# In odd attention heads the values product by three passes of rounded parts, and the next head's keys ahead of the third scores

## What is computed

```python
kv = (key_ckv @ p["w_ukv"]).reshape(B, M, N_HEADS, QK_NOPE + V_DIM)
k_nope, v = kv[..., :QK_NOPE], kv[..., QK_NOPE:]
...
s = jnp.einsum("bqhd,bkhd->bhqk", qi, k).astype(jnp.float32) * scale
p = jax.nn.softmax(s, axis=-1).astype(v.dtype)
return jnp.einsum("bhqk,bkhd->bqhd", p, v)
```

## Time and profile before

| | |
|---|---|
| median of 3 runs | 2737.5 us (2736.6 to 2740.0) |
| the profiled execution | 2737.6 us, its span 2735.8 us |
| one head in steady order | 17.9 us |
| the eight heads of layer 1, from the first Exp to the end of head 7 | 135.7 us |
| mean granted TensorE clock | 0.993 of full speed |

### The profile page before, as it was taken

The page is one execution under the profiler, slowest core; times in us unless marked ns, Lnnn a source line. Parts: engine busy times, 40 slices in busy tenths (PEclk is TensorE's granted clock), DMA queues, the critical chain, the costliest instruction groups (busy, mean ns, idle before and its releaser), DMA issues. The chain is left out here.

```text
span 2735.8 us, 44480 instructions
## 1 busy us (share of the span) xinstructions
PE 2664.7 (97%) x17686; PEld 2524.1 (92%) x17686; DVE 2092.7 (76%) x2832; ACT 1213.6 (44%) x2002; POOL 626.7 (23%) x327
## 2 busy tenths in 40 slices
PE   5999999999999999999999999999999999999997
PEld 3999999977899999999989999999779999999997
DVE  6978879776567788887888879888665668786876
ACT  5533425556432543343564435355663245343433
POOL 1322412023000124232322413310220003232230
PEclk9999999999999999999999999999999999999999
DMA  6434232211233253423324243322113322222312
GB/s 233 158 119 135 85 124 73 70 44 32 74 128 102 95 170 113 132 99 104 101 99 154 93 133 106 110 62 70 30 37 115 126 83 78 93 80 68 109 47 77
DMA packets 87693, 270.90 MB, mean 99 GB/s; under 512 B 8704, under 2 KB 12544, under 8 KB 87360
## 3 DMA queue, kind: packets, MB, share of 16 engines
q1 hardware_dynamic: 86048, 263.51, 29.3%
q10 hardware_dynamic: 1440, 4.56, 0.5%
HBM read 265.12 MB, written 2.92 MB: 98 GB/s over the span
## 5 line engine op out<-in xcount | busy, mean ns | idle before, releaser
L690 POOL TENSOR_TENSOR sums_raw<-raw_pairs 128x1024 f32<-128x1024 f32 x88 | 238.3, 2708 | 1618.6 <-DVE weights_lo L1822 1032.9
L725 PE MATMUL ps<-h_hi,weights_hi 128*128 128x322 f32 (+1 forms) x1408 | 440.3, 313 | 8.9 <-DVE t_lo L1822 3.1
L729 PE MATMUL ps<-h_hi,weights_lo 128*128 128x322 f32 (+1 forms) x1408 | 437.1, 310 | 0.0
L727 PE MATMUL ps<-h_lo,weights_hi 128*128 128x322 f32 (+1 forms) x1408 | 436.6, 310 | 0.0
L1822 DVE TENSOR_TENSOR weights_lo<-sums_raw,weights_hi 128x1024 fp32r<-128x1024 f32 (+2 forms) x296 | 329.8, 1115 | 57.1 <-ACT weights_hi L1344 27.1
L725 PE MATMUL ps<-t_hi,weights_hi 128*128 128x322 f32 (+1 forms) x1056 | 330.4, 313 | 5.3 <-DVE h_lo L1822 5.3
L725 PE MATMUL ps<-a_hi,weights_hi 128*128 128x320 f32 x1408 | 325.1, 312 | 5.3 <-DVE tmp L2024 3.6
L729 PE MATMUL ps<-t_hi,weights_lo 128*128 128x322 f32 (+1 forms) x1056 | 327.4, 310 | 0.0
L727 PE MATMUL ps<-t_lo,weights_hi 128*128 128x322 f32 (+1 forms) x1056 | 326.3, 309 | 0.0
L727 PE MATMUL ps<-a_lo,weights_hi 128*128 128x320 f32 x1408 | 321.4, 309 | 0.0
L729 PE MATMUL ps<-a_hi,weights_lo 128*128 128x320 f32 x1408 | 321.2, 309 | 0.0
(11 more groups left out here) (288 smaller groups left out, 5750.9 us busy)
## 6 DMA issues: line engine op xcount, KB each, us to landing
raw_pairs<-in_w_up SPq DMA_DIRECT2D x87, 1024.0 KB, 5.0
wm<-in_w_mod SPq DMA_DIRECT2D x72, 512.0 KB, 4.0
raw<-in_w_merge SPq DMA_DIRECT2D x32, 704.0 KB, 4.1
sums_raw<-in_w_down SPq DMA_DIRECT2D x56, 384.0 KB, 3.2
sums_raw<-in_w_down SPq DMA_DIRECT2D x64, 320.0 KB, 3.0
wm<-in_w_mod SPq DMA_DIRECT2D x48, 256.0 KB, 3.0
raw<-in_w_in SPq DMA_DIRECT2D x16, 512.0 KB, 3.5
late_wm<-in_w_mod SPq DMA_DIRECT2D x16, 512.0 KB, 3.5
```

The lines of the kernel that those rows point to most:

```text
L690: nc.gpsimd.tensor_tensor(sums_raw[:, UNIT:3 * UNIT].rearrange("p (s c) -> p s c", s=2), w.rearrange("p (s c) -> p s c", s=2)[:, :, 0:UNIT ...
L725: nc.tensor.matmul(out, whi, v, start=first, stop=False)
L727: nc.tensor.matmul(out, whi, v, start=False, stop=False)
L729: mm = nc.tensor.matmul(out, wlo, v, start=False, stop=last)
```

## The change

Head by head it does the following.

- In odd heads `values(j)` becomes three passes: v1 (values rounded, and ones) x the rounded exponentials, the values' lo part (64 result rows) x the rounded exponentials, and v1 x the exponentials' lo part. It waits for VectorE's subtraction (`s_vxlo`) in place of the Exp.
- In odd heads `exponent(j)` issues two Exps, one to the rounded buffer `ex_parts(h, j)[0]`, one to the float32 buffer `ex[j % 2]`. For j of 2 and more it also waits for `exponent_lo(j - 2)`. `exponent_lo(hd, j)` on VectorE subtracts the rounded from the float32 exponentials. The parts lie in columns of the weight slots that a head's chunk leaves free; for head 7 in q0 and a view over `tmp`.
- `values_lo` on VectorE makes the lo part of an odd head's values from PSUM, before the last maximum of the even head.
- v1 is rounded and has the values first, the ones last, written by ScalarE once a layer; GpSimd's memset of v1 goes. `o_copy` takes its rows accordingly.
- The order of odd heads changes on TensorE (keys and values of the next head ahead of `scores(2)`; `values(j)` after `scores(j + 2)`), on ScalarE (`keys` ahead of the third Exp, `values_copy` ahead of the fourth, `split_queries` after the fourth) and on VectorE (subtractions between the maxima). Even heads keep theirs but for `values_lo`.

```diff
+        with ExitStack() as of_last:
+            last_parts = sb("last_parts", [P, 6 * T + 4], F32R, of_last)
...
-                    v1 = sb("v1", [P, KEYS // P, P], F32, head)
+                    v1 = sb("v1", [P, KEYS // P, P], F32R, head)
...
+        def ex_parts(h, j):
+
+            n = SAMPLE if j < 6 else P
+            if h == HEADS - 1 and j % 2:
+                return q0_hi[:, 0:n], q0_lo[:, 0:n]
+            if h == HEADS - 1:
+                return last_parts[:, 2 * SAMPLE:2 * SAMPLE + n], last_parts[:, 2 * SAMPLE + 2 * T:2 * SAMPLE + 2 * T + n]
+            at = 3 * UNIT * (j % 2) + SLOT - SAMPLE
+            return mix_w_hi[:, at:at + n], mix_w_lo[:, at:at + n]
+
+        def value_lo_parts(h):
+
+            if h == HEADS - 1:
+                return last_parts[:, 2 * SAMPLE + T:2 * SAMPLE + T + 4 * VD],                     last_parts[:, 2 * SAMPLE + T + 4 * VD:2 * SAMPLE + T + 7 * VD]
+            return mix_w_hi[:, HEAD_W:HEAD_W + 4 * VD], mix_w_lo[:, HEAD_W:HEAD_W + 3 * VD]
+
+        def value_lo_done(hd):
+            return hd // 2 * 8 + 1
+
+        def ex_lo_done(hd, j):
+            return hd // 2 * 8 + 2 + j
...
-                for s in range(2):
-                    nc.gpsimd.memset((v0, v1)[s][:, :, (1 - s) * VD:(2 - s) * VD], 1.0).then_inc(s_fill, 1)
-                    pool.wait_ge(s_fill, 7 + 2 * l + s + 1)
+                nc.gpsimd.memset(v0[:, :, VD:2 * VD], 1.0).then_inc(s_fill, 1)
+                pool.wait_ge(s_fill, 7 + l + 1)
...
                 if hd % HEADS and not tail:
                     pe.wait_ge(s_v, hd)
+                    if hd % 2 == 0:
+                        pe.wait_ge(s_vxlo, value_lo_done(hd - 1))
...
-                    pe.wait_ge(s_exp, t0 + j + 1)
-                    out, v_in = (bank(7), ex[j % 2]) if j < 6 else (bank(1 if following else 3, 0, P), ex[j % 2][:, 0:P])
-                    nc.tensor.matmul(out, vals[b][:, j, :], v_in, start=j in (0, 6), stop=j in (5, 6)).then_inc(s_pv, 1)
+                            pe.wait_ge(s_fill, 7 + l + 1)
+                    out = bank(7) if j < 6 else bank(1 if following else 3, 0, P)
+                    if b:
+                        pe.wait_ge(s_vxlo, ex_lo_done(hd, j))
+                        e_hi, e_lo = ex_parts(h, j)
+                        value_lo = value_lo_parts(h)[j // 4][:, j % 4 * VD:(j % 4 + 1) * VD]
+                        nc.tensor.matmul(out, v1[:, j, :], e_hi, start=j in (0, 6), stop=False)
+                        nc.tensor.matmul(out[0:VD], value_lo, e_hi, start=False, stop=False)
+                        nc.tensor.matmul(out, v1[:, j, :], e_lo, start=False, stop=j in (5, 6)).then_inc(s_pv, 1)
+                    else:
+                        pe.wait_ge(s_exp, t0 + j + 1)
+                        v_in = ex[j % 2] if j < 6 else ex[j % 2][:, 0:P]
+                        nc.tensor.matmul(out, v0[:, j, :], v_in, start=j in (0, 6), stop=j in (5, 6)).then_inc(s_pv, 1)
...
+                if b:
+                    if following:
+                        pe.wait_ge(s_rowc, hd + 1)
+                        keys_values(c1 % 2, QT)
+                    scores(2)
+                    values(0)
+                    scores(3)
+                    values(1)
+                    scores(4)
+                    if following:
+                        rough(hd + 1, 0, 2)
+                    values(2)
+                    if following:
+                        rough(hd + 1, 1, 2)
+                        turn_values(hd + 1)
+                        rough(hd + 1, 2, 2)
+                    scores(5)
+                    values(3)
+                    if following:
+                        rough(hd + 1, 3, 2)
+                    scores(6)
+                    values(4)
+                    if following:
+                        rough(hd + 1, 4, 2)
+                    values(5)
+                    values(6)
+                    if following:
+                        maximum_rows(hd + 1)
+                    return
...
+                one_rows = ones[:, 0:VD]
+                nc.scalar.activation(v1[:, :, VD:P], bass.AP(one_rows.tensor, one_rows.offset,
+                                                             [one_rows.ap[0], (0, KEYS // P), (1, VD)]), ACT.Copy)
...
             def o_copy(hd):
                 s = hd % 2
-                o_rows, s_rows = slice(s * VD, (s + 1) * VD), slice((1 - s) * VD, (2 - s) * VD)
+                o_rows = slice(s * VD, (s + 1) * VD)
                 act.wait_ge(s_pv, (hd + 1) * 7)
                 act.wait_ge(s_olo, hd // 2)
-                for dst, rows in ((o32, o_rows), (sums, s_rows)):
+                for dst, rows in ((o32, slice(0, VD)), (sums, slice(VD, P))):
...
+                    if h % 2:
+                        if j >= 2:
+                            act.wait_ge(s_vxlo, ex_lo_done(hd, j - 2))
+                        nc.scalar.activation(ex_parts(h, j)[0], bank(j % 2, 0, n), ACT.Exp)
                     nc.scalar.activation(ex[j % 2][:, 0:n], bank(j % 2, 0, n), ACT.Exp).then_inc(s_exp, 1)
 
                 if following:
                     queries(hd + 1)
                 exponent(0)
                 exponent(1)
+                if h % 2:
+                    weight_hi(2 * mixp + HEADS_C + h + 2)
+                    if following:
+                        keys(hd + 1, mixp, head_chunk(h + 1))
+                    exponent(2)
+                    if following:
+                        values_copy(hd + 1)
+                    exponent(3)
+                    if following:
+                        split_queries(hd + 1)
+                    exponent(4)
+                    if following:
+                        values(hd + 1)
+                    exponent(5)
+                    exponent(6)
+                    if following:
+                        maximum_hi(hd + 1)
+                    o_copy(hd)
+                    if following:
+                        maximum_copy(hd + 1)
+                    return
...
-                for h in range(HEADS):
-                    if h and h % 2 == 0:
+                nc.vector.tensor_copy(k1_lo[NOPE:QK + 2, :], k0_lo[NOPE:QK + 2, :].bitcast(F32)).then_inc(s_krlo, 1)
+                for h in range(0, HEADS, 2):
+                    if h:
                         o_norm(l, h // 2 - 1)
                     weight_lo(c0 + HEADS_C + h + 2)
-                    if h and h % 2 == 0:
+                    if h:
                         o_lo(l, h // 2 - 1)
-                    if h + 1 < HEADS:
-                        split_queries(hd0 + h + 1)
-                        split_keys(hd0 + h + 1)
-                        for u in range(UNITS):
-                            maximum(hd0 + h + 1, u)
-                        maximum_lo(hd0 + h + 1)
+                    split_queries(hd0 + h + 1)
+                    split_keys(hd0 + h + 1)
+                    for u in range(UNITS):
+                        if u == UNITS - 1:
+                            values_lo(hd0 + h + 1)
+                        maximum(hd0 + h + 1, u)
+                    maximum_lo(hd0 + h + 1)
+                    odd, following = hd0 + h + 1, h + 2 < HEADS
+                    exponent_lo(odd, 0)
+                    weight_lo(c0 + HEADS_C + h + 3)
+                    exponent_lo(odd, 1)
+                    exponent_lo(odd, 2)
+                    if following:
+                        split_keys(odd + 1)
+                    exponent_lo(odd, 3)
+                    if following:
+                        maximum(odd + 1, 0)
+                        split_queries(odd + 1)
+                        maximum(odd + 1, 1)
+                    exponent_lo(odd, 4)
+                    if following:
+                        maximum(odd + 1, 2)
+                        maximum(odd + 1, 3)
+                    exponent_lo(odd, 5)
+                    if following:
+                        maximum(odd + 1, 4)
+                    exponent_lo(odd, 6)
+                    if following:
+                        maximum_lo(odd + 1)
...
+            def values_lo(hd):
+                dve.wait_ge(s_v, hd + 1)
+                for to, first, last in zip(value_lo_parts(hd % HEADS), (0, 4), (4, 7)):
+                    ins = lo_of(to.rearrange("p (a n) -> p a n", n=VD),
+                                bank(4, first * VD, last * VD).rearrange("p (a n) -> p a n", n=VD), v1[:, first:last, 0:VD])
+                ins.then_inc(s_vxlo, 1)
+
+            def exponent_lo(hd, j):
+                e_hi, e_lo = ex_parts(hd % HEADS, j)
+                dve.wait_ge(s_exp, hd * 7 + j + 1)
+                lo_of(e_lo, ex[j % 2][:, 0:SAMPLE if j < 6 else P], e_hi).then_inc(s_vxlo, 1)
```

More of the change, by code:

```diff
@@ L368, in build @@
         q_hi, q_lo = [q0_hi, ot_hi[:, OT - 1, :]], [q0_lo, ot_lo[:, OT - 1, :]]
-        k_hi, k_lo, vals = [k0_hi, k1_hi[:]], [k0_lo[:], k1_lo[:]], [v0, v1]
+        k_hi, k_lo = [k0_hi, k1_hi[:]], [k0_lo[:], k1_lo[:]]
```

(36 more changed lines are left out.)

## The result

The changed kernel takes 2761.45 us (median of 5 runs, 2757.24 to 2764.32), the kernel before 2737.5: the ratio is 1.0087, with a 95% interval of 1.0076 to 1.0098. It is slower, as predicted, by 24 us where 28.5 was forecast. The profiled execution took 2759.8 us, its span is 2757.8.

A forecast was written before the change was run, and what follows sets the result against it. TensorE, busy 97% of the span, was taken as the bound. To 2737.6 us came +23.4 (odd heads +15.2, head 7 +6.6, even heads +1.6) and +5.1 for the clock: 2766 us, range 2751 to 2777.

The forecast's parts named there:

- the walk: Step-by-step timing of an odd head across the engines, giving TensorE waits of 1.35, 1.39 and 0.91 us.
- values(5): Third wait of an odd head: VectorE's row of maxima and subtractions ends 16.13, TensorE arrives 15.38; 0.91 us.
- First wait: Odd head, before values(1): second subtraction delayed by GpSimd's rotations at the shared port; 1.35 us.
- Second wait: Odd head, before rough(0): the queries' rounding stands behind the fourth Exp pair, which waits for values(1)'s buffer; 1.39 us.
- Gain: TensorE, values blocks of odd heads: three rounded passes replace the full-precision product, saving 0.8 us per odd head.
- Keys: Odd heads with a follower: keys ahead of the third scores cover TensorE's 0.32 us wait before values(0).
- Odd head +2.53: Net per odd head with a follower: three waits less passes and keys, +2.53 us; six give +15.2.
- Even heads +0.2: VectorE's low part of the values, before the last maximum, makes TensorE wait 0.2 us per even head; eight, +1.6.
- Head 7 +3.3 each: Last head of each layer: values(1) waits 2.45, doubled Exps add 0.41, 0.36, 0.78; net +3.3 us, two +6.6.
- The clock: TensorE's clock drops in most of eight odd heads, at half of 1.7 us each: 6.8 less 1.7, +5.1.
- A granted clock under 1 in most odd heads: Expected sign in the profile after: TensorE's clock lowered in most odd heads; staying at 1.00 would refute the forecast.
- Rival C: Clock falls in every odd head at full price, +11.9 us, giving 2773 us or more; chance 0.15.

The follow-up runs named there:

- experiment 4: Changed kernel without GpSimd's three rotations in odd heads (queries of heads 2, 4, 6 stay unrotated): 2759.3 us, ratio to the kernel before 1.0081.
- experiment 1: Changed kernel with VectorE's second subtraction of exponentials ahead of the weight subtraction in odd heads: 2760.2 us, ratio to the kernel before 1.0082.
- experiment 2: Changed kernel with ScalarE's rounding of the next head's queries ahead of the fourth Exp pair in odd heads: 2754.2 us, ratio to the kernel before 1.0063.
- experiment 5: Changed kernel without second Exp and subtractions, third pass reusing the rounded Exps, queries rounded ahead of the fourth Exp: 2736.4 us, ratio to the kernel before 0.9996.
- experiment 6: Kernel before with only the next head's keys moved to the front in odd heads (TensorE, ScalarE, VectorE): 2735.7 us, ratio 0.9995.
- experiment 11: Changed kernel, odd heads' queues reordered, head 7 in full precision, keys first in even heads too, values' low part behind the last maximum: 2735.5 us, ratio 0.9996.
- experiment 10: Kernel before with the next head's keys moved ahead in every head that has a follower, even ones too: 2733.7 us, ratio 0.9986.
- experiment 9: Changed kernel with head 7 of each layer alone kept at the full-precision values product, one Exp, no subtractions: 2756.8 us, ratio to the kernel before 1.0066.
- experiment 3: Changed kernel with both reorderings, VectorE's second subtraction ahead of the weight subtraction and ScalarE's query rounding ahead of the fourth Exp pair: 2750.7 us, ratio 1.0050.

## Why the prediction was right, and where it was off

**The sign and the mechanism were right.** All three waits stand where the walk put them, with the releasers it named. Late by the reading above, against the walk: values(1) 1.13 (1.35), rough(0) 1.41 (1.39), values(5) 0.85 (0.91).

- **First wait, mis-sized by 0.2.** The turns at the port came earlier than walked, the end of the third rotation 6.32 us in, not 6.53; values(1) began 0.37 earlier (0.2 of it from the rotation, the rest from a shorter step from the rotation's end to the product, 0.60 against 0.76), and its slow first pass, left out of the walk, gave back 0.1. Its cause, GpSimd ahead of a queued subtraction, is shown by experiment 4: with no rotation the second subtraction takes 0.69 in place of some 2. The page "SBUF — State Buffer" of the Trainium skill, section "Who interferes with whom", calls the port pair that VectorE and GpSimd share an exclusive lock; the trace agrees, with 1.29 us for the weight subtraction beside the rotations against 0.82 without them.
- **Second wait.** 1.41 against 1.39, as two misses cancel: the chain from the end of values(1) to rough(0) took 2.00, not 2.09, and the slow first pass, 0.1, was left out. That the fourth Exp pair waits for the buffer of values(1) is seen on ScalarE: in the changed kernel it starts 0.25 behind the end of values(1), 0.44 after the copy of the values. In experiment 1, with values(1) on time, it starts right behind that copy, 7.56 us in instead of 7.98. So the buffer holds it up by 0.42 only, and rough(0) then comes 0.41 earlier; the rest is what stands ahead of the rounding in ScalarE's queue, as experiment 2 shows. ScalarE, head 1, in the changed kernel and then in experiment 1 (first scores at 600.71 and 601.13):

```profile
607.28 0.97 ACT L1747 ACTIVATE tmp<-ps 64x448 f32<-64x448 f32 x2
608.69 0.60 ACT L1791 ACTIVATE mix_w_hi<-ps 128x512 fp32r<-128x512 f32 x1 [0.44 <-issue]
```

```profile
608.69 0.60 ACT L1791 ACTIVATE mix_w_hi<-ps 128x512 fp32r<-128x512 f32 x1
```

- **Gain, mis-sized.** The passes were put at 0.80 a head. A block takes 0.69, and three passes of 128 columns 0.23, not 3 x 0.11: together 6 x (0.86 - 0.69) - 0.03 = 0.99; experiments 5 and 6 give 0.9. Keys 0.32 forecast, 0.28 measured.
- **Odd head +2.53 forecast, +2.03 measured.** Of the 0.5, 0.26 are the waits and 0.1 to 0.2 the passes; the rest isn't placed. In six heads this is 3.0 of the 4.5 us between forecast and result.
- **Even heads +0.2 forecast, +0.10 to +0.17 measured.** Experiment 11 beside experiment 10 shows the cause: behind the last maximum the low part costs 0.03.
- **Head 7 +3.3 each.** In layer 2 values(1) is late by 2.37 (2.45 forecast), scores(2) by 0.41 (0.41), values(5) by 1.1 (0.36 + 0.78). The third comes in one piece; the clock fell in between.

```profile
2073.24 0.50 PE L749 MATMUL ps<-ot_hi,k_hi 98*128 98x512 f32 x1
...
2075.30 0.40 PE L753 MATMUL ps<-ot_hi,k_lo 98*128 98x512 f32 x1
2077.80 0.49 PE L1241 MATMUL ps<-q_hi,v 128*128 128x512 f32 x1 [2.10 <-DVE q_lo L1913]
...
2085.05 0.50 PE L1241 MATMUL ps<-q_hi,v 128*128 128x512 f32 x1 [0.86 <-DVE q_lo L1913]
```

```profile
2074.00:2078.00 4.00, 1.90 (x8) 1.21 (x8) 2.49 (x3) 2.45 (x4) 0.00 (x0) 1.00 0.55 218
2078.00:2082.00 4.00, 4.00 (x12) 2.97 (x12) 1.03 (x2) 1.71 (x4) 0.00 (x0) 0.58 0.52 180
```

Timeline and windows of the changed kernel, head 7 of layer 2, to set beside the earlier trace rows: 2.10 us idle at full clock, then 4 us at 0.58. From 2078.59 on nine passes take 3.65 us in place of 9 x 0.23 = 2.07. That is 1.6 of the 4.75 by which the head grew; 3.2 are left for the waits less the gain, where 3.3 was forecast. In layer 1 the clock fell early, as in the kernel before, and the slow passes filled the wait: 0.64 recorded in place of 2.10, and the head grew by 1.67 alone.

- **The clock, the term that came out by luck.** The forecast had eight falls at 0.85, half of 1.7, so 6.8, less the 1.7 already in the time before: net 5.1. In the profile they come to 3.9 in head 3, 1.6 in head 7 of layer 2 and 0.1 in head 7 of layer 1, so 5.6, less the 1.6 of the kernel before: net 4.0, with 19.8 left for the heads at full clock, where 23.4 was forecast. Both factors of the 6.8 were wrong, and the errors cancelled. The price of 1.7 was read at head 7, where slowed passes are over after 4 us and fill later waits; in an odd head the lower clock lasted 7 to 10 us and cost 3.2 to 3.9 (23.1 to 23.9 against 19.95). And it fell in 3 of 12 odd heads (the changed kernel and experiment 9), not in most: the forecast's sign "A granted clock under 1 in most odd heads" didn't show. Rival C, a fall in every head, priced so (six odd heads at 3.6, two of 1.6 in head 7, less 1.7), would have been some 11 us dearer than it was.

## What to carry to other kernels

An engine with half its time free is no cover by itself: list for each product the queue that its newest operand comes through and what stands ahead of it there, shared ports among it. Here that order set the waits and, with them, the falls, 24 us together, and reordering alone gave it back. Removing one wait of a chain pays only down to the next late operand, and can cost when it gathers short waits into one long one. Try the order change by itself first: of this change it was the only part that paid in any order tried. An order in which the passes reach the estimated 16.7 us was not found.

## What of the hardware was not expected

**At nearly the same sum of idle, the clock fell with some cuts of it and not with others.** Odd heads with a follower, recorded waits of one head at full clock, and heads that fell, in one profiled execution of each kernel:

| runs | waits in a head, us | sum | heads that fell |
|---|---|---|---|
| experiments 2, 3 | 0.89, 0.47, 1.01 and 0.79, 0.46, 1.06 | 2.3 to 2.4 | 0 of 12 |
| changed kernel, experiment 9 | 0.87, 1.16, 0.57 | 2.6 | 3 of 12 |
| experiments 1, 4 | 1.76, 0.55 and 1.75, 0.78 | 2.3 to 2.5 | 8 of 12 |

The share of heads that fell rises with the longest single wait (1.07 at most, 1.16, 1.76 us) and not with the sum. A fall cost 1.5 to 3.0 us in experiments 1 and 4, where it began later in the head, and up to 3.9 in the others. The Trainium skill, page "TensorE: Matmul & The Clock Gate", section "Why this matters for your kernels", warns only of idle gaps longer than any of these; here one of 1.76 was followed by a fall in most heads. The longest wait is not the whole of it, since head 7 falls in some runs after 0.78 and 0.58 alone. Why the same gap makes the clock fall in one head and not in the next, these runs don't show; nor was a kernel tried in which only the cut of the idle differs. Head 7 falls or not from run to run with unchanged waits of 0.78 and 0.58 (12.4 or 10.75 us), which alone moves the time by up to 3.3 us.

**Three passes of 128 columns take 0.23 us** (617.43 to 617.66), where two of the kernel before took 0.22: the first ones lie only 0.06 and 0.05 apart.
